# Entry of the output stage: who makes the low parts of the output weights, and when

## The chip, the cores and the metric

The kernel runs on one core of a Trainium2 chip. The metric is the time of one execution on the device in microseconds. Five engines work side by side, each through its own list of instructions: TensorE (PE in the profile), VectorE (DVE), ScalarE (ACT), GpSimd (POOL) and SyncE (SP), which here only issues transfers. They meet by semaphores: an instruction waits until a counter has reached a value, and adds to a counter when it is done.

## The reference

One layer of a diffusion backbone, for 256 prompt tokens and 2048 sample tokens, width 1024, float32:

```
h = RMSNorm(x) * (1 + scale1) + shift1
q, k, v, r, decays, conv inputs = split(h @ w_in)
A = per-head RMSNorm(gated linear attention, both directions) * norm_g * silu(r)   # 512 wide, 4 heads
B = silu(LayerNorm(depthwise conv, width 31, of ga * sigmoid(gg)))                  # 512 wide
x = x + gate1 * (concat(A, B) @ w_out)                                              # w_out: 1024 x 1024
h = RMSNorm(x) * (1 + scale2) + shift2
x = x + gate2 * ExpertChoiceMoE(h)                                                  # 16 experts
y = RMSNorm(x)
```

Outputs are y of both token sets and the final states of the two attention scans of the prompt.

## The kernel before

**Products in two parts.** Each float32 operand of a large product is split into a high part (a rounded copy, `ACT.Copy` by ScalarE into a tile of type fp32r) and a low part (the operand less its high part, a `tensor_tensor` subtraction by VectorE or GpSimd). `three` (lines 1649 to 1652) then runs three matmuls: high by high, high by low, low by high.

**Stages.** Stage 2 projects the tokens and runs attention and convolution, first for the prompt and then for four blocks of 512 sample tokens. It parks its results in HBM (`park_q`, `park_s` for states, `park_o`, `park_r`, `park_c` for the convolution). Stage 3 takes them back in five groups m = 0 to 4: group 0 is the prompt (256 tokens, two tiles of 128), groups 1 to 4 are the blocks, last block first (512 tokens, four tiles each). It finishes the norms, multiplies by the output weights, adds the residual and computes the router's logits. Stage 4 runs the experts. The change is at the entry of stage 3, in the `prologue` of each engine, which prepares group 0 and the output weights; `stage3(m)` then computes group m while it prepares group m + 1.

**Order.** Nothing is scheduled by a planner: each engine's instructions run in the order in which the code writes them. What stands behind a waiting instruction on its engine waits too.

**The output weights.** `wo_hl[:, 0, k, :]` and `wo_hl[:, 1, k, :]` are the high and low part of k-slice k (k = 0 to 7, each 128x1024). SyncE loads w_out in four transfers of two slices (1 MB each) into the three buffers `wstage` (which later hold x rows, scaled rows and h2 of stage 3); the fourth goes into buffer 0 once slices 0 and 1 are split. `wo_hi(k)` (line 1139, ScalarE) makes a high part and raises `r_wh`. `wo_lo(k)` (line 2711, VectorE) waits for it, makes the low part and raises `r_wl`.

**VectorE's prologue** (lines 2716 to 2730): `centre(0)` (2627), `taps` 108 to 117 of the last block's convolution (2560), `add_inter(0)` (2635), `taps` 118 to 123, `wo_lo` 0 to 3, `gate_heads(0)` (2642, four multiplications of 128x256), `wo_lo` 4 and 5, `stat_recips(0)` (2647 a reciprocal, 2649 its low part), `wo_lo` 6 and 7, `scale_all(0)` (2657 the four heads, 2663 the convolution's four quarters), a copy (2730).

**ScalarE's prologue**: squares of the convolution (1067), `wo_hi` 0 and 1, the gate rows (1149), `wo_hi` 2 and 3, squares of the heads (1074), `wo_hi` 4 and 5, `stat_roots(0)` (1079, a square root of sums that TensorE made), `stat_hi(0)` (1087, waits for the reciprocal), `wo_hi` 6 and 7, `cat_his(0)` (1100 high parts of attention, 1093 the convolution's silu, 1100 high parts of the convolution).

**GpSimd** makes the low parts of attention and convolution, `cat_lo` (1454). Before its first one in stage 3 it has only four memsets (1469 to 1473).

**TensorE's prologue**: sums of squares (1922, 1926), `spread(0)` (1939, spreads the reciprocals over the partitions into PSUM). Then `out_half(g, q)` multiplies tile g by half q of the weights, 24 matmuls of 128x512; the first one waits for `r_wl` slice by slice. Behind the 48 matmuls of tile 0 come `conv_mean(1)` (1914, waits for `park_c` of group 1) and `inter(1)` (1904, the product of queries and states, waits for `back_states(1)`, line 2611, on VectorE, which waits for the parked states).

**SyncE** at this place, in its order: three loads of w_out, `load_r(0)`, the store of the prompt's state, `store_c(final)` (622, the last block's convolution, waits for all its taps), a wait for two low parts, the fourth load of w_out (718), `load_qS(1)` (633 queries, 637 and 638 states), `load_r(1)`, a wait for all eight low parts, the x rows of tiles 0 and 1 (673), then `load_c(1)` and `load_o(1)` (645, 651), which wait for the low parts of group 0.

Of the kernel before, what the change touches and what calls it, by code (L numbers as in the profile page):

```python
# [41 lines left out]
TAPS = 4 * CW  # L42
# [56 lines left out]
def hybrid_layer(nc, x_prompt, x_sample, state_gla_fwd, state_gla_bwd, c, c_ctx, norm_mix_g, norm_ffn_g,  # L99
# [3 lines left out]
    f32, f32r, bf16, u32 = mybir.dt.float32, mybir.dt.float32r, mybir.dt.bfloat16, mybir.dt.uint32  # L103
    f16 = mybir.dt.float16
    ALU = mybir.AluOpType
# [3 lines left out]
    with ctx:  # L109
# [66 lines left out]
        with ExitStack() as st:  # L176
            wo_hl = group(st, "wo_hl", [128, 2, KC, D], f32r)
# [213 lines left out]
        r_x2st, r_h2st = [sem("r_x2st0"), sem("r_x2st1")], [sem("r_h2st0"), sem("r_h2st1")]  # L391

        P_AFF, P_COPY = 5, 7

        def upto(eng, sig_, n):

            eng.wait_ge(sig_.sem, sig_.base + n)
# [127 lines left out]
        def _(sp):  # L525
# [192 lines left out]
            sp.dma_start(wstage[0], wo_v[3]).then_inc(r_wo[0].sem, 16)  # L718
            load_qS(1)
            load_r(1)  # L720
            sp.wait_ge(r_wl, 8)
            load_x3(0)
            load_x3(1)
            for m in range(NBLK + 1):
# [106 lines left out]
        def _(act):  # L831
# [244 lines left out]
            def stat_roots(m):  # L1076
                act.wait_ge(r_st, 2 * m + 2)
                wait_pos(act, r_bc, 5 * m)
                act.activation(W3["rs"][0:64, 0:T3[m]], psum[7][0:64, 0:T3[m]], ACT.Sqrt, bias=eps[0:64, :],
                               scale=1.0 / DV).then_inc(r_sr, 1)  # L1080

            def stat_hi(m):
                act.wait_ge(r_rc, m + 1)
                wait_pos(act, r_bc, 5 * m)
                if m == 0:
                    act.wait_ge(r_sel, 4)
                act.activation(spread_rs[0:64, 0:T3[m]], W3["rs"][0:64, 0:T3[m]], ACT.Copy).then_inc(r_sh.sem, 1)
# [48 lines left out]
            def prologue():  # L1136
                def wo_hi(k):
                    upto(act, r_wo[k // 2 % 3], 32 if k >= 6 else 16)
                    act.activation(wo_hl[:, 0, k, :], wstage[k // 2 % 3][:, k % 2, :], ACT.Copy).then_inc(r_wh, 1)

                for j in range(16):
                    act.activation(diag[:, j, :], ident[:, :], ACT.Copy, scale=mod[:, 16 + j % 8, j // 8:j // 8 + 1])\
                       .then_inc(r_dg, 1)
                conv_squares(0)
                wo_hi(0)
                wo_hi(1)
                for j in range(4):
                    act.wait_ge(r_gt, j + 1)
                    act.activation(gt1[:, j // 2, 512 * (j % 2):512 * (j % 2) + 512], psum[j][:, :], ACT.Copy)\
                       .then_inc(r_gr, 1)  # L1150
                wo_hi(2)
                wo_hi(3)
                head_squares(0)
                upto(act, r_mt, 1)
                act.activation(mod2_rows, psum[4][0:2 * KC, 0:256], ACT.Copy).then_inc(r_mt.sem, 1)
                wo_hi(4)
                wo_hi(5)
                stat_roots(0)
                stat_hi(0)
                wo_hi(6)  # L1160
                wo_hi(7)
                cat_his(0)
# [205 lines left out]
        def _(pool):  # L1368
# [105 lines left out]
            def routing_constants():  # L1474
# [27 lines left out]
                for out, pattern, cm in ((iota_a[:, :], [[16, 16]], 0), (iota_b[:, :], [[1, 16]], 0),  # L1502
                                         (iota_p[:, :], [[1, CAPP]], 0), (lat_id[:, :], [[128, NL]], 1),
                                         (pr_id[:, :, :], [[128, 2], [0, 2]], 1)):
                    chain(pool.iota(out, pattern, base=0, channel_multiplier=cm, allow_small_or_imprecise_dtypes=True))

            for m in range(NBLK + 1):
                for half in range(2):
                    if m == 0:
                        final.wait(pool, s_conv if half == 0 else s_cstr, TAPS if half == 0 else s_cstr.l)  # L1510
                    for t in range(min(NT3[m], 3)):
                        cat_lo(m, t, half)
                if NT3[m] == 4:
                    cat_lo(m, 3, 0)
                    cat_lo(m, 3, 1)
                if m == 1:
                    routing_constants()
# [120 lines left out]
        def _(pe):  # L1638
# [305 lines left out]
            def out_half(g, q, k0=0, k1=KC):  # L1944
                m = M_OF[g]
                t = g - G3[m]
                if g >= 2 and k0 == 0:
                    pe.wait_ge(r_y, 2 * (g - 2) + q + 1)
                elif q == 0 and k0 == 0:
                    pe.wait_ge(r_gr, 4)  # L1950
                for k in range(k0, k1):
                    if g == 0 and q == 0:
                        pe.wait_ge(r_wl, k + 1)
                    if q == 0 and k % 4 == 0:
                        upto(pe, r_lo, piece(m, t, k // 4))
                    a = cat_hl[:, :, k, 128 * t:128 * t + 128]
                    last = three(psum[2 * (g % 2) + q][:, :], a[:, 0], a[:, 1], wo_hl[:, 0, k, 512 * q:512 * q + 512],
                                 wo_hl[:, 1, k, 512 * q:512 * q + 512], k == 0, k == KC - 1)
                if k1 == KC:
                    last.then_inc(r_T.sem, 1)  # L1960
# [369 lines left out]
        def _(dve):  # L2330
# [368 lines left out]
            def prologue():  # L2699
# [14 lines left out]
                centre(0)  # L2714
                taps(final, LATE, 118)
                add_inter(0)
                taps(final, 118, TAPS)
                wo_lo(0)
                wo_lo(1)
                wo_lo(2)  # L2720
                wo_lo(3)
                gate_heads(0)
                wo_lo(4)
                wo_lo(5)
                stat_recips(0)
                wo_lo(6)
                wo_lo(7)
                scale_all(0)
                dve.wait_ge(r_br, 1)
                dve.tensor_copy(brow_w, psum[5][:, 0:2 * NE]).then_inc(r_wr, 1)  # L2730

# [538 lines left out]
```

## Time and profile before

| | us |
|---|---|
| median of 3 runs | 2403.95 (2400.47 to 2404.53) |
| the profiled execution | 2401.75, of which the profiled span is 2400.0 |
| TensorE busy in the span | 2240.2 (93%) |
| VectorE, ScalarE, GpSimd busy | 1667.6, 1193.9, 721.8 |

Times in the rows are microseconds from the start of the span. Engines wait for each other, so an engine's busy time says little by itself; the timelines show an instruction's start and length and, in brackets, the idle time ahead of it and what ended it. Tiles of the three stages bear the names of their regions: work_proj (stage 2), work_out (stage 3), work_exp (stage 4); bank is a PSUM bank. PEclk is the clock granted to TensorE, 1.00 for 2.4 GHz and 0.50 for 1.2 GHz. The DMA share is the mean busy share of the 16 DMA engines.

### The profile page before, as it was taken

To read this page: it belongs to the slowest core of one execution; us is meant where nothing else is said; L and a number is where in the kernel's file an instruction comes from. 1 tells how busy PE (TensorE), PEld (TensorE's weight loads), DVE (VectorE), ACT (ScalarE), POOL (GpSimd) and SP (SyncE) were. 2 spreads that over 40 slices of the span, in tenths; PEclk is the share of its full clock that TensorE was granted. 3 is DMA by queue.
4 is the path that set the end of the run, shared out by engine and by line. 5 is a ranking of instruction groups with operands and counts; after the bars stand their busy time and mean duration, and the time that the engine had idled before them with its cause. 6 is when DMAs were issued, how large, how long until landed. Compare 5 with 4: busy or idle time off the path is not lost.

```text
span 2400.0 us, 43832 instructions
## 1 busy us (share of the span) xinstructions
PE 2240.2 (93%) x16687; PEld 2053.6 (86%) x16687; DVE 1667.6 (69%) x2936; ACT 1193.9 (50%) x1935; POOL 721.8 (30%) x663
## 2 busy tenths in 40 slices
PE   4889999999996899975999999999999999999995
PEld 4778878788885677753999999999999999999995
DVE  2879979799788766767666655665656656666585
ACT  3765363553524454432545554555445554555574
POOL 2000000000001311101254455544554455544551
PEclk8999999999997999987999999999999999999998
DMA  8986677657747566355476677667776677666986
GB/s 297 347 292 217 219 245 248 238 184 273 221 131 265 166 203 198 102 178 139 151 206 193 184 199 214 188 183 200 198 214 183 176 213 198 207 184 185 299 253 241
DMA packets 289654, 505.79 MB, mean 211 GB/s; under 512 B 26178, under 2 KB 232895, under 8 KB 273921
## 3 DMA queue, kind: packets, MB, share of 16 engines
q1 hardware_dynamic: 249622, 376.39, 47.9%
q0 software_dynamic: 39424, 126.64, 19.5%
q8 instruction: 78, 1.28, 0.2%
q10 hardware_dynamic: 490, 1.16, 0.1%
q14 instruction: 40, 0.32, 0.0%
HBM read 405.61 MB, written 98.53 MB: 210 GB/s over the span
## 4 chain that ended last, share of the span: by engine, by line
PE 61%; DVE 5%; ACT 2%; issue 1%; DMA 1%; POOL 0%; SPq 0%; DVEq 0%; POOLq 0%; ACTq 0%
PE bank L1650 19%; PE bank L1652 19%; PE bank L1651 19%; PE bank L1904 1%; DVE work_exp L2921 1%; DVE work_proj L2560 1%; PE bank L1970 1%; PE bank L1914 1%; PE bank L1922 1%; DMA work_exp<-x_rows 0%; POOL cat_hl L1454 0%; PE bank L1979 0%; PE bank L2213 0%; DVE wo_hl L2711 0%; ACT hl_exp L1231 0%
## 5 line engine op out<-in xcount | busy, mean ns | idle before, releaser
L1650 PE MATMUL bank<-act_hl_exp,hl_exp 128*128 128x288 f32 x3072 | 909.2, 296 | 12.2 <-DVE hl_exp L3100 7.3
L1651 PE MATMUL bank<-act_hl_exp,hl_exp 128*128 128x288 f32 x3072 | 906.5, 295 | 0.0
L1652 PE MATMUL bank<-act_hl_exp,hl_exp 128*128 128x288 f32 x3072 | 905.0, 295 | 0.0
L1650 PEld LDWEIGHTS bank<-act_hl_exp,hl_exp 128*128 128x128 f32 x3072 | 576.7, 188 | 13.7 <-DVE hl_exp L3100 9.8
L1652 PEld LDWEIGHTS bank<-act_hl_exp,hl_exp 128*128 128x128 f32 x3072 | 578.6, 188 | 0.0
L1651 PEld LDWEIGHTS bank<-act_hl_exp,hl_exp 128*128 128x128 f32 x3072 | 577.3, 188 | 0.0
L3100 DVE TENSOR_TENSOR hl_exp<-work_exp,hl_exp 128x1024 fp32r<-128x1024 f32 x192 | 231.3, 1226 | 206.1 <-ACT hl_exp L1231 206.1
L3100 DVE TENSOR_TENSOR hl_exp<-raw_exp,hl_exp 128x1024 fp32r<-128x1024 f32 x192 | 232.0, 1225 | 193.3 <-ACT hl_exp L1231 193.3
L2560 DVE SCALAR_TENSOR_TENSOR work_proj<-work_proj,wcv 128x392 f32<-128x392 f32 (+12 forms) x600 | 338.8, 635 | 1.2
L1231 ACT ACTIVATE hl_exp<-work_exp 128x1024 fp32r<-128x1024 f32 x192 | 199.2, 1054 | 201.3 <-PE bank L1652 201.3
L1231 ACT ACTIVATE hl_exp<-raw_exp 128x1024 fp32r<-128x1024 f32 x192 | 198.5, 1052 | 161.5 <-PE bank L1652 161.5
L1565 POOL TENSOR_TENSOR act_hl_exp<-work_exp,act_hl_exp 128x288 fp32r<-128x288 f32 x128 | 155.5, 1234 | 360.0 <-ACT act_hl_exp L1257 360.0
L1588 POOL DMA_INDIRECT x_rows<-work_exp x135 | 241.6, 1790 | 60.3 <-issue 36.0
L1650 PE MATMUL bank<-act_hl_proj,hl_proj 128*128 128x512 f32 (+1 forms) x640 | 239.4, 374 | 6.0 <-DVE hl_proj L2387 6.0
L1651 PE MATMUL bank<-act_hl_proj,hl_proj 128*128 128x512 f32 (+1 forms) x640 | 234.9, 367 | 0.0
L1652 PE MATMUL bank<-act_hl_proj,hl_proj 128*128 128x512 f32 (+1 forms) x640 | 234.7, 367 | 0.0
L1427 POOL DMA_DIRECT2D hl_proj<-park_w x80 | 43.3, 542 | 602.0 <-PE bank L1652 511.2
L1553 POOL DMA_INDIRECT work_exp<-h_rows,work_exp x135 | 162.0, 1200 | 50.0 <-issue 38.3
L1242 ACT ACTIVATE work_exp<-work_exp 128x256 f32<-128x256 f32 x240 | 102.3, 497 | 90.3 <-DVE work_exp L3111 64.0
L1650 PEld LDWEIGHTS bank<-act_hl_proj,hl_proj 128*128 128x128 f32 x640 | 123.3, 193 | 27.2 <-issue 8.7
L1652 PEld LDWEIGHTS bank<-act_hl_proj,hl_proj 128*128 128x128 f32 x640 | 123.0, 192 | 19.6
L1651 PEld LDWEIGHTS bank<-act_hl_proj,hl_proj 128*128 128x128 f32 x640 | 123.3, 193 | 17.8
(411 smaller groups left out, 3317.4 us busy)
## 6 DMA issues: line engine op xcount, KB each, us to landing
hl_proj<-park_w POOLq DMA_DIRECT2D x80, 1024.0 KB, 6.1
raw_exp<-in_w_e_gate_dram SPq DMA_DIRECT2D x32, 1024.0 KB, 5.9
raw_exp<-in_w_e_up_dram SPq DMA_DIRECT2D x32, 1024.0 KB, 5.8
work_exp<-in_w_e_gate_dram SPq DMA_DIRECT2D x32, 1024.0 KB
work_exp<-in_w_e_up_dram SPq DMA_DIRECT2D x32, 1024.0 KB, 6.5
raw_exp<-in_w_e_down_dram SPq DMA_DIRECT2D x32, 1024.0 KB, 6.2
work_exp<-in_w_e_down_dram SPq DMA_DIRECT2D x32, 1024.0 KB, 5.8
park_w<-hl_proj SPq DMA_DIRECT2D x8, 2048.0 KB, 12.0
```

What stands on the lines that cost most here:

```text
L1231: act.activation(half_out(j, q, 0, is_last(e)), half_in(src, j, q, is_last(e)), ACT.Copy).then_inc(s_hi, 1)
L1242: last = act.activation(h32e[:, k % 2, a:z], xT[:, k % 2, a:z], ACT.Identity, scale=A2q[:, cnd, k:k + 1], bias=sh2q[:, cnd, k:k + 1])
L1427: pool.dma_start(hl[:, j % 2, q], park_w[j, :, q]).then_inc(s_w[j % 2][q].sem, 16)
L1553: pool.indirect_dma_start(xg[:, b, :], None, h2_rows[:, :], bass.IndirectOffsetOnAxis(ap=ids_g[:, b:b + 1], axis=0)).then_inc(e_gat, 16)
L1565: pool.tensor_tensor(xe_hl[:, 1, k, :], h32e[:, k % 2, :], xe_hl[:, 0, k, :].bitcast(f32), ALU.subtract)\
L1588: pool.indirect_dma_start(x2_quarters[:, :], bass.IndirectOffsetOnAxis(ap=ids_s[:, b:b + 1], axis=0), y_t[:, b, :], None, compute_op=ALU.a ...
L1650: pe.matmul(out, lh, rh, start=first, stop=False)
L1651: pe.matmul(out, lh, rl, start=False, stop=False)
L1652: return pe.matmul(out, ll, rh, start=False, stop=last_)
L1904: ins = pe.matmul(psum[7 - h % 2][v:v + 64, 64 * cc:64 * cc + 64], S3[:, cc + 1, 128 * h + v:128 * h + v + 64], part("q", m, h)[:, 64 * cc ...
L2560: dve.scalar_tensor_tensor(out=ac[:, :, a0:a1], in0=uu[:, :, a0 + off:a1 + off], scalar=wcv[:, ct, w:w + 1], in1=ac[:, :, a0:a1], op0=ALU. ...
L3100: dve.tensor_tensor(half_out(j, q, 1, is_last(e)), half_in(src, j, q, is_last(e)), half_out(j, q, 0, is_last(e)).bitcast(f32), ALU.subtrac ...
```

## The change

GpSimd makes the low parts of slices 2 to 5, with a counter of its own (`r_wlp`, on a semaphore that has reached 20 by then), in order and ahead of its first `cat_lo`; each waits for its high part. VectorE makes the low parts of slices 0 and 1 ahead of its last six taps, and those of 6 and 7 behind `scale_all(0)`. ScalarE makes high part 4 between `stat_roots(0)` and `stat_hi(0)`, and high part 5 behind it. TensorE and SyncE wait for both counters.

```diff
--- before.py
+++ after.py
@@ -391,6 +391,7 @@
         r_x2st, r_h2st = [sem("r_x2st0"), sem("r_x2st1")], [sem("r_h2st0"), sem("r_h2st1")]
 
         P_AFF, P_COPY = 5, 7
+        r_wlp = Sig(s_cst, 0, 0, 20)
 
         def upto(eng, sig_, n):
 
@@ -718,7 +719,8 @@
             sp.dma_start(wstage[0], wo_v[3]).then_inc(r_wo[0].sem, 16)
             load_qS(1)
             load_r(1)
-            sp.wait_ge(r_wl, 8)
+            sp.wait_ge(r_wl, 4)
+            upto(sp, r_wlp, 4)
             load_x3(0)
             load_x3(1)
             for m in range(NBLK + 1):
@@ -1153,10 +1155,10 @@
                 head_squares(0)
                 upto(act, r_mt, 1)
                 act.activation(mod2_rows, psum[4][0:2 * KC, 0:256], ACT.Copy).then_inc(r_mt.sem, 1)
+                stat_roots(0)
                 wo_hi(4)
+                stat_hi(0)
                 wo_hi(5)
-                stat_roots(0)
-                stat_hi(0)
                 wo_hi(6)
                 wo_hi(7)
                 cat_his(0)
@@ -1504,6 +1506,10 @@
                                          (pr_id[:, :, :], [[128, 2], [0, 2]], 1)):
                     chain(pool.iota(out, pattern, base=0, channel_multiplier=cm, allow_small_or_imprecise_dtypes=True))
 
+            for k in range(2, 6):
+                pool.wait_ge(r_wh, k + 1)
+                pool.tensor_tensor(wo_hl[:, 1, k, :], wstage[k // 2 % 3][:, k % 2, :], wo_hl[:, 0, k, :].bitcast(f32),
+                                   ALU.subtract).then_inc(r_wlp.sem, 1)
             for m in range(NBLK + 1):
                 for half in range(2):
                     if m == 0:
@@ -1949,8 +1955,10 @@
                 elif q == 0 and k0 == 0:
                     pe.wait_ge(r_gr, 4)
                 for k in range(k0, k1):
-                    if g == 0 and q == 0:
-                        pe.wait_ge(r_wl, k + 1)
+                    if g == 0 and q == 0 and 2 <= k < 6:
+                        upto(pe, r_wlp, k - 1)
+                    elif g == 0 and q == 0:
+                        pe.wait_ge(r_wl, k + 1 if k < 2 else k - 3)
                     if q == 0 and k % 4 == 0:
                         upto(pe, r_lo, piece(m, t, k // 4))
                     a = cat_hl[:, :, k, 128 * t:128 * t + 128]
@@ -2714,18 +2722,14 @@
                 centre(0)
                 taps(final, LATE, 118)
                 add_inter(0)
-                taps(final, 118, TAPS)
                 wo_lo(0)
                 wo_lo(1)
-                wo_lo(2)
-                wo_lo(3)
+                taps(final, 118, TAPS)
                 gate_heads(0)
-                wo_lo(4)
-                wo_lo(5)
                 stat_recips(0)
+                scale_all(0)
                 wo_lo(6)
                 wo_lo(7)
-                scale_all(0)
                 dve.wait_ge(r_br, 1)
                 dve.tensor_copy(brow_w, psum[5][:, 0:2 * NE]).then_inc(r_wr, 1)
```

## Rows read from the trace of the kernel before

**Rows 1.** The page: chain that ended last, share of the span by engine.
```profile
PE 61%; DVE 5%; ACT 2%; issue 1%; DMA 1%; POOL 0%; SPq 0%; DVEq 0%; POOLq 0%; ACTq 0%
```

**Rows 2.** Timeline, VectorE: start us, length us, engine, line, op, output<-inputs, count [idle before<-releaser].
```profile
741.72 3.36 DVE L2560 SCALAR_TENSOR_TENSOR work_proj<-work_proj,wcv 128x408 f32<-128x408 f32 x6
...
744.99 4.62 DVE L2711 TENSOR_TENSOR wo_hl<-work_out,wo_hl 128x1024 fp32r<-128x1024 f32 x4
...
749.53 1.43 DVE L2642 TENSOR_TENSOR work_out<-work_out 128x256 f32<-128x256 f32 x4
...
753.15 1.73 DVE L2647 RECIPROCAL work_out<-work_out 64x256 f32<-64x256 f32 x1
...
758.59 0.87 DVE L2657 SCALAR_TENSOR_TENSOR work_out<-work_out,col,bank 128x256 f32<-128x256 f32 x2
...
760.89 1.42 DVE L2663 TENSOR_TENSOR work_out<-work_out,bank 128x256 f32<-128x256 f32 x4 [0.28 <-PE bank L1939]
...
766.96 0.60 DVE L2605 COPY work_out<-carry 64x512 f32<-64x512 f32 x1 [4.55 <-DMA work_out<-park_s]
...
767.59 10.42 DVE L2611 SCALAR_TENSOR_TENSOR work_out<-work_out,dec 64x128 f32<-64x128 f32 x32
```

**Rows 3.** Timeline of ScalarE, from 744 to 762 us.
```profile
744.06 2.01 ACT L1139 ACTIVATE wo_hl<-work_out 128x1024 fp32r<-128x1024 f32 x2
...
751.03 0.47 ACT L1079 ACTIVATE work_out<-bank,eps 64x256 f32<-64x256 f32 x1
...
760.65 1.15 ACT L1100 ACTIVATE cat_hl<-work_out 128x512 fp32r<-128x512 f32 x2 [3.42 <-DVE work_out L2657]
```

**Rows 4.** Timeline of GpSimd, from 728 to 764 us.
```profile
761.43 2.50 POOL L1454 TENSOR_TENSOR cat_hl<-work_out,cat_hl 128x512 fp32r<-128x512 f32 x2 [33.89 <-ACT cat_hl L1100]
```

**Rows 5.** Timeline of TensorE's matmuls, from 746 to 780 us.
```profile
746.43 0.40 PE L1926 MATMUL bank<-work_out 128*32 128x256 f32 x1 [2.56 <-ACT work_out L1074]
...
748.09 1.06 PE L1926 MATMUL bank<-work_out 128*32 128x256 f32 x2
...
762.84 0.77 PE L1650 MATMUL bank<-wo_hl,cat_hl 128*128 128x512 f32 x1 [1.99 <-POOL cat_hl L1454]
...
776.41 3.59 PE L1914 MATMUL bank<-work_out,ones 128*128 128x512 f32 x8
```

**Rows 6.** Timeline of SyncE's queue: the issues of transfers, 745 to 769 us.
```profile
745.11 0.34 SPq L622 DMA_DIRECT2D park_c<-work_proj  x1
...
747.37 0.37 SPq L718 DMA_DIRECT2D work_out<-in_w_out_dram  x1
...
768.73 0.33 SPq L645 DMA_DIRECT2D work_out<-park_c  x1
```

**Rows 7.** Stretches: length, busy us of each engine (instructions), PEclk, DMA share, GB/s.
```profile
745.50:775.00 29.50, 20.76 (x77) 15.54 (x78) 23.17 (x47) 13.89 (x22) 5.21 (x4) 0.65 0.99 315
...
747.60:768.00 20.40, 12.59 (x39) 9.30 (x36) 14.24 (x23) 11.81 (x17) 4.52 (x4) 0.50 1.00 282
```

**Rows 8.** Transfers issued at 745.11, 747.37, 768.73: KB, us from issue to landing.
```profile
park_c<-work_proj SPq DMA_DIRECT2D x1, 1024.0 KB, 4.1
...
work_out<-in_w_out_dram SPq DMA_DIRECT2D x1, 1024.0 KB, 5.7
...
work_out<-park_c SPq DMA_DIRECT2D x1, 1024.0 KB, 6.2
```

**Rows 9.** Timelines of GpSimd and VectorE, at 43 us and from 813 us.
```profile
43.27 2.49 POOL L1422 TENSOR_TENSOR act_hl_proj<-work_proj,act_hl_proj 128x1024 fp32r<-128x1024 f32 x1 [1.94 <-ACT act_hl_proj L898]
...
44.18 2.67 DVE L2378 TENSOR_TENSOR act_hl_proj<-work_proj,act_hl_proj 128x1024 fp32r<-128x1024 f32 x1 [0.62 <-ACT act_hl_proj L898]
...
813.91 6.55 POOL L1454 TENSOR_TENSOR cat_hl<-work_out,cat_hl 128x512 fp32r<-128x512 f32 x5 [2.20 <-ACT cat_hl L1100]
...
815.31 1.38 DVE L2611 SCALAR_TENSOR_TENSOR work_out<-work_out,dec 64x128 f32<-64x128 f32 x1
```

**Rows 10.** Groups of ScalarE by line: table load, mean ns, idle before, releaser.
```profile
L855 ACT ACT_TABLE_LOAD x1 | 1.3, 1283 | 15.8 <-DVE col L2333 15.8
```

## Prediction

> **What bounds the kernel now.** I began with the chain of work that ended last. TensorE has 61% of it [rows 1], so the entry of stage 3 matters only as far as it holds TensorE up. Then I read the timelines of this entry, engine by engine, to see what releases TensorE.
>
> VectorE runs without a break: the six last convolution taps from 741.72 to 745.0, low parts 0 to 3 from 744.99 (4.62 us), the head gating, then low parts 4 and 5, the reciprocal, low parts 6 and 7, and the head scaling from 758.59 [rows 2]. ScalarE makes the first high part of attention at 760.65 [rows 3], GpSimd its low part from 761.43 [rows 4], and TensorE starts on the output matmuls at 762.84, having idled 1.99 us for GpSimd [rows 5]. The 48 matmuls of tile 0 and what follows run without a gap until conv_mean(1), 776.41 to 780.0 [rows 5]. This is the chain that the change wants shorter.
>
> A second chain runs beside it. SyncE waits for the last tap before it stores the convolution (issue 745.11), and behind that store stand, in its queue, the fourth part of the output weights (747.37) and all the loads of group 1 [rows 6]. From 745.5 to 775 the DMA engines are busy 0.99 of the time [rows 7]. They serve SyncE's transfers in the order of issue: the store lands after 4.1 us, at 749.2, the fourth part at 753.1, the convolution of group 1 at 774.9 [rows 6, 8]. The parked states of group 1 stand two transfers ahead of the x rows in the same queue: VectorE idles 4.55 us for it until 766.96 and needs 0.60 and 10.42 us for the backward states [rows 2], to 778.04. TensorE reaches conv_mean(1) only 1.5 us after its data landed (776.41 less 774.9), and the head product behind it at 780.0, 1.9 us after the states. So whatever the first chain gains, this second one takes over within 1.5 us; and whatever delays the store beyond that delays TensorE.
>
> **The change part by part.**
>
> *VectorE.* Low parts 0 and 1 move ahead of the taps: 2 x 1.155 = 2.31 us (4.62 / 4) [rows 2]. The first begins at 741.72, as its high part was ready. The taps then begin at 744.03 and end at 747.35 if nothing disturbs them (6 in 3.3 us). That alone moves the store by 2.35 us.
>
> *GpSimd.* It gets four differences of 128x1024. The trace has one such: 2.49 us [rows 9]. The first may start when ScalarE has made high part 2, 1.0 us after 744.06, at 745.1 [rows 3]. That is among the taps. What this does to VectorE is seen twice. While the 128x1024 difference ran from 43.27 to 45.76, a VectorE difference of the same size, started at 44.18, took 2.67 us instead of 1.16 (it ended 1.1 us behind GpSimd's). And among the five differences that GpSimd makes from 813.91, VectorE's 64x128 state step took 1.38 us (815.31), against 10.42 / 32 = 0.33 us in rows 2, so one VectorE step passed for each of GpSimd's (6.55 / 5 = 1.31 us) [rows 2, 9]. VectorE's work whose second input is a PSUM bank did not suffer: four at 760.89 in 1.42 us while GpSimd worked from 761.43 [rows 2, 4]. The taps and the gating have both inputs in SBUF, so I take them as blocked.
>
> The Trainium skill (SBUF — State Buffer, section Who interferes with whom) says the same as a rule: VectorE with two SBUF inputs and a GpSimd instruction that reads SBUF contend, and the second fully blocks until the first is done. The trace agrees (2.67 us at 44.18). If the two ran freely side by side, the taps would cost nothing more; that is rival A.
>
> Played through: GpSimd begins at 745.15, after tap 2. Tap 3 waits until 747.65 and runs 0.55; GpSimd's second runs 748.2 to 750.7; taps 4, 5, 6 run from 750.7 to 752.35. If tap 3 wins the first race, the sum is the same: two blocks of 2.5 us inside the taps. So the taps end at 744.03 + 3.3 + 5.0 = 752.35. GpSimd's third difference needs high part 4. ScalarE now makes it after the roots, which need TensorE's sums at 749.2 and a table load of 1.28 us [rows 10]. The load stands behind its wait where that can be seen (15.8 us of idle ahead of one) [rows 10]. The sums are two matmuls of 0.5 us at 748.1 [rows 5]; the root takes 0.5 us and the high part 1.0 [rows 3]. That gives 749.2 + 1.28 + 0.5 + 1.0 = 752.0: just too late for the taps, but it blocks the gating by another 2.5 us. Gating ends at 754.85 + 1.43 = 756.3, the reciprocal (1.73) at 758.0, the head scaling starts at about 759.6, 1.0 us later than now. The low parts taken out of this chain (4 x 1.16 us) are so given back by 3 blocks of 2.5 us.
>
> *SyncE.* The store is issued at 752.45, 7.3 us later than 745.11. The engines lie idle meanwhile. Everything behind moves by 7.3 us, less up to 0.6 us of thin traffic between the issues before: 6.7 to 7.3. The fourth part lands at 760.5 (752.45 + 4.1 + 3.9). ScalarE needs 2 x 1.0 us for high parts 6 and 7 ahead of the attention's, which so comes at 762.5 instead of 760.65 [rows 3]: TensorE starts 1.8 us later than 762.84 and comes free for conv_mean(1) at 778.2. VectorE's low parts 6 and 7, now behind the scaling, are ready by 768.3; TensorE wants them 18 matmuls after its start, about 772. No cost. GpSimd's fourth difference (759.5 to 762.0) is done before the attention's high part. No cost. The new waits of SyncE (x rows of group 0) fall under transfers that queue until 776; no cost.
>
> *Where it decides.* The convolution of group 1 lands at 774.9 + 6.7 to 7.3 = 781.6 to 782.2, so conv_mean(1) starts 5.2 to 5.8 us later than 776.41. The other input agrees: the state lands at 773.7 to 774.3, the backward states end 11.1 us later, 784.8 to 785.4, against a head product at 780.0 before: 4.8 to 5.4 later. I take 5.5. Nothing behind it is tied to an earlier time: all loads and steps of the later groups are released by steps of this one, so the delay stays to the end.
>
> *The clock.* TensorE will idle about 4 us ahead of conv_mean(1). Its granted clock was 0.50 (1.2 GHz) from 747.6 to 768 [rows 7], after 2.56 us of idle ahead of 746.43 [rows 5]. conv_mean's eight matmuls take 3.59 us at 2.4 GHz; at half of it they cost up to 3.5 us more, at best nothing. I take the middle, 1.6.
>
> **Sum:** 5.5 + 1.6 = +7.1 us. The profiled execution took 2401.75 us (span 2400.0 and 1.75 around it), which becomes 2408.9. The median of the runs is 2403.95, 2.2 above it, so I forecast 2411.0. Its own range: 4.8 + 0 to 5.8 + 3.5, so 2408.8 to 2413.3.
>
> **The rivals.**
>
> A. *No block.* GpSimd and VectorE run side by side on the taps. For it: TensorE's and PSUM-fed work is undisturbed; against it rows 9. Then the taps end at 747.35, the store goes 2.35 us later, the convolution lands at 777.3, 0.9 us later than 776.41; the states end at 780.4, 0.4 later than 780.0. TensorE waits from 773.3 on (as in C), so the clock may cost 0 to 3.5 as well. Time 2404.9, up to 2408.
>
> B. *A third block inside the taps.* If high part 4 is ready before 751.8 (the table loaded ahead of the wait), GpSimd's third difference gets in before taps 5 and 6. One more 2.5 us: +9.6, 2413.6. Rows 10 speak against it.
>
> C. *The change does what it says* and the second chain does not bind. High parts 6 and 7 wait for the fourth part (753.1 + 2.4 = 755.5), the attention's high part comes at 757.5 instead of 760.65: 3.1 us gained, 2400.8; TensorE starts at 759.7 and is through with tile 0 at 773.3 (776.41 less 3.1). It decides this way only if conv_mean's data land before 773.3, though the store goes later and the DMA engines are full [rows 7]. I see nothing for that.
>
> **How the numbers follow.** Forecast 0.62, A 0.22, B 0.12, C 0.04. The predicted time is the forecast's, 2411.0. The range goes from A to just above B, 2404.9 to 2414.0: outside lie C, the lowest times of A and the upper half of B, below 2 in 10. About 0.2% (4.8 us) is what a measurement of this kernel can tell from no change, so the border is at 2408.8. Slower: the forecast less its low end (0.57), B (0.12) and a little of A (0.02), 0.71. Within: A (0.20), C (0.03), the forecast's low end (0.04), 0.27. Faster 0.02.
>
> **What would show it.** In the profile of the changed kernel: two of the last six taps last some 3 us each, a gating step some 2.5; the convolution's store is issued near 752.4; conv_mean(1) starts near 782 behind a wait for the DMA of the convolution, with a granted clock of 0.50 for some us. It is wrong if the taps keep 0.55 us each, if the store is issued by 748, or if the transfers behind it land no later than before.

## The result

| | before | after |
|---|---|---|
| median of 6 runs, us | 2399.93 (2397.47 to 2404.53) | 2410.42 (2406.9 to 2413.86) |
| profiled execution, us | 2401.75 (span 2400.0) | 2412.79 (span 2411.1) |

The ratio is 1.0042 (95% interval 1.0027 to 1.0057), so the change costs 10.1 us (6.5 to 13.7). The time forecast, 2411.0, is near the measured one; the change forecast, 7.1 us, is too small by 3.0. The two don't say the same because the kernel before came out 4.0 us lower in six runs than in the three that the forecast stood on. The change in us is what the reasons have to answer for, and there a rival that I had given 0.12 is what happened. The kernel before was timed again beside the experiments: its medians there are 2401.86, 2400.24 and 2401.82, and 2410.42 is 8.6 to 10.2 us above these; the traces below give 9.6.

**The chain that ended last, in the changed kernel** (start us, length us, what), at the entry of stage 3:

```profile
741.96 2.27 DVE wo_hl L2719 x2
744.22 4.37 DVE work_proj L2568 x5
...
751.08 2.71 DVE work_proj L2568
...
753.80 0.34 SPq L623
...
754.19 7.20 DMA work_out<-in_w_out_dram
...
761.41 2.00 ACT wo_hl L1141 x2
...
771.19 13.12 DMA work_out<-park_c
...
784.35 5.40 PE bank L1920 x8
```

Read it from below. TensorE's conv_mean(1) waits for the convolution of group 1 (13.12 us from issue to landing); its issue waits for GpSimd's low parts of the prompt, these for ScalarE, which makes high parts 6 and 7 first and waits for the fourth weights (7.20 us), and these stand in SyncE's queue behind the store at 753.80, which waits for the last tap. In the kernel before, the chain went through the norms to TensorE's first output matmul. It now goes through the store and two transfers. The 13.12 us are mostly queueing: from the store's issue to the landing of the convolution the DMA engines are busy 0.99 of the time, and this takes 30.5 us, against 29.8 in the kernel before (745.11 to 774.9).

The three taps that lost time, in VectorE's timeline, and what GpSimd did then:

```profile
745.79 2.73 DVE L2568 SCALAR_TENSOR_TENSOR work_proj<-work_proj,wcv 128x400 f32<-128x400 f32 x1
...
748.45 2.71 DVE L2568 SCALAR_TENSOR_TENSOR work_proj<-work_proj,wcv 128x392 f32<-128x392 f32 x1
...
751.08 2.70 DVE L2568 SCALAR_TENSOR_TENSOR work_proj<-work_proj,wcv 128x392 f32<-128x392 f32 x1
```

```profile
745.36 2.73 POOL L1511 TENSOR_TENSOR wo_hl<-work_out,wo_hl 128x1024 fp32r<-128x1024 f32 x1 [17.68 <-ACT wo_hl L1141]
...
748.06 2.67 POOL L1511 TENSOR_TENSOR wo_hl<-work_out,wo_hl 128x1024 fp32r<-128x1024 f32 x1
...
751.01 2.35 POOL L1511 TENSOR_TENSOR wo_hl<-work_out,wo_hl 128x1024 fp32r<-128x1024 f32 x1 [0.28 <-ACT wo_hl L1141]
```

Each tap ends 0.4 us behind the end of a difference of GpSimd's: 748.52 behind 748.09, 751.16 behind 750.73, 753.78 behind 753.36. In these rows it gets its turn only when that difference is through, and the next difference then takes the turn ahead of the next tap. The six taps take 9.64 us, against 3.36 in [rows 2]. The other lines of TensorE and VectorE that answer to [rows 5] and [rows 2] (SyncE's, for [rows 6], stand in the chain above: 753.80, 754.19 and 771.19):

```profile
766.13 0.76 PE L1656 MATMUL bank<-wo_hl,cat_hl 128*128 128x512 f32 x1 [5.51 <-POOL cat_hl L1456]
...
784.35 5.40 PE L1920 MATMUL bank<-work_out,ones 128*128 128x512 f32 x8 [4.50 <-DMA work_out<-park_c]
789.68 1.15 PE L1910 MATMUL bank<-work_out 128*64 128x64 f32 x32
```

```profile
776.43 0.42 DVE L2613 COPY work_out<-carry 64x512 f32<-64x512 f32 x1 [11.46 <-DMA work_out<-park_s]
```

TensorE's late start (766.13 against 762.84) is the store's doing too. VectorE's head scaling is not late: it begins 17.3 us behind the second pair of head additions (line 2643, at 741.06), against 17.7 before. ScalarE waits for the fourth weights:

```profile
761.41 2.00 ACT L1141 ACTIVATE wo_hl<-work_out 128x1024 fp32r<-128x1024 f32 x2 [3.24 <-DMA work_out<-in_w_out_dram]
```

The landings behind 753.80 and 771.19, and four stretches (the columns of [rows 7]):

```profile
park_c<-work_proj SPq DMA_DIRECT2D x1, 1024.0 KB, 5.0
...
work_out<-park_c SPq DMA_DIRECT2D x1, 1024.0 KB, 13.1
```

```profile
745.50:775.00 29.50, 17.64 (x63) 13.00 (x64) 17.32 (x21) 13.92 (x22) 15.59 (x8) 0.60 0.70 190
...
753.80:784.00 30.20, 16.07 (x53) 12.08 (x53) 16.38 (x42) 8.91 (x13) 8.02 (x5) 0.71 0.99 307
...
780.00:784.30 4.30, 0.00 (x0) 0.00 (x0) 4.16 (x15) 0.00 (x0) 0.00 (x0) 1.00 1.01 417
...
785.00:788.00 3.00, 3.00 (x5) 1.20 (x4) 1.80 (x6) 0.00 (x0) 0.00 (x0) 0.50 0.04 16
```

The DMA share from 745.5 to 775 fell from 0.99 to 0.70: the engines had nothing to do until the store came. TensorE idles 4.50 us. Its granted clock still stands at 1.00 from 780 to 784.3, without a matmul, and is 0.50 (1.2 GHz) from 785 to 788, when the matmuls run again: conv_mean(1) takes 5.40 us instead of 3.59.

What is lost there stays lost. The head product is 9.75 us later (789.68 against 779.93), and the first matmul of the experts 9.8 us later: 1134.4 to 1144.2, in the group of these matmuls of before and of after (nanoseconds least/median/most, first and last start in us):

```profile
L1650 PE MATMUL bank<-act_hl_exp,hl_exp x3072: 288/295/607, 1134.4 to 2378.2; 128*128 128x288 f32 x192
```

```profile
L1656 PE MATMUL bank<-act_hl_exp,hl_exp x3072: 288/295/609, 1144.2 to 2388.8; 128*128 128x288 f32 x192
```

### The profile page after: what moved, and what is told of

The parts are those of the page before. It is cut to its first block, busy times and chain, and to the rows that moved or that the text cites. A ratio compares the mean times of both kernels' runs of the same rounds, so it can differ in the third digit from the quotient of the medians.

```text
span 2411.1 us, 43833 instructions
## 1 busy us (share of the span) xinstructions
PE 2243.5 (93%) x16687; PEld 2056.0 (85%) x16687; DVE 1669.3 (69%) x2932; ACT 1193.9 (50%) x1935; POOL 732.9 (30%) x667
## 3 DMA queue, kind: packets, MB, share of 16 engines
q0 software_dynamic: 39424, 126.64, 19.5%
## 4 chain that ended last, share of the span: by engine, by line
PE 60%; DVE 4%; DMA 3%; ACT 1%; issue 1%; POOL 1%; SPq 0%; DVEq 0%; ACTq 0%; POOLq 0%
PE bank L1656 19%; PE bank L1658 18%; PE bank L1657 18%; DMA out_dram<-work_exp 1%; PE bank L1910 1%; DMA work_out<-park_c 1%; PE bank L1920 1%; PE bank L1978 1%; DVE work_exp L2925 1%; DVE work_proj L2568 1%; PE bank L1928 1%; DVE work_exp L3188 0%; POOL cat_hl L1456 0%; DMA work_exp<-x_rows 0%; PE bank L2149 0%
## 5 line engine op out<-in xcount | busy, mean ns | idle before, releaser
L2568 DVE SCALAR_TENSOR_TENSOR work_proj<-work_proj,wcv 128x392 f32<-128x392 f32 (+12 forms) x600 | 345.2, 647 | 1.2
L1658 PEld LDWEIGHTS bank<-act_hl_proj,hl_proj 128*128 128x128 f32 x640 | 122.9, 192 | 19.5
```

Source lines behind the costliest of these rows:

```text
L1658: return pe.matmul(out, ll, rh, start=False, stop=last_)
L2568: dve.scalar_tensor_tensor(out=ac[:, :, a0:a1], in0=uu[:, :, a0 + off:a1 + off], scalar=wcv[:, ct, w:w + 1], in1=ac[:, :, a0:a1], op0=ALU. ...
```

## The experiments

Theory: GpSimd's differences block VectorE's taps whole instructions at a time, so the store at the head of all transfers of group 1 goes out late, and TensorE waits for the last of them and then runs for a while at half its clock. Main rival: the norms' chain, or rather TensorE's late start on the output matmuls (766.13, 3.3 us later), is what costs. The trace of the changed kernel speaks against it already: TensorE waits 4.50 us for the data after the late start.

Executions enter the stage up to 1.2 us earlier or later, so I measure each trace from the start of VectorE's second pair of head additions (line 2635; 740.91 in the kernel before) to the start of the head product, the matmul behind conv_mean(1). This is 39.0 us before. "First matmul" is TensorE's first output matmul, counted from the pair as well. Each trace is one execution, and executions of one kernel differ by some 10 us over the whole (kernel before, 2395.85 to 2407.08), so the traces say where time is lost and the timed column says how surely. e2 and e5 ran once each, for their traces: 2402.4 and 2411.21 us, beside medians of 2401.86 and 2400.24 for the kernel before.

| kernel | pair, us | first matmul, after the pair | head product, us | between | against before | timed against before, us (interval) |
|---|---|---|---|---|---|---|
| before | 740.91 | 21.9 | 779.93 | 39.0 | | |
| changed | 741.06 | 25.1 | 789.68 | 48.6 | +9.6 | +10.1 (6.5 to 13.7) |
| e1, GpSimd after the taps | 741.06 | 19.5 | 782.89 | 41.8 | +2.8 | +2.2 (-0.5 to 5.0) |
| e2, GpSimd only writes | 740.46 | 18.1 | 782.58 | 42.1 | +3.1 | |
| e3, store behind all loads | 739.72 | 21.6 | 785.86 | 46.1 | +7.1 | +4.8 (2.4 to 7.2) |
| e4, lows first, no GpSimd | 741.51 | 25.2 | 784.79 | 43.3 | +4.3 | +2.6 (0 to 5.5) |
| e5, high part 4 later | 742.14 | 23.2 | 789.97 | 47.8 | +8.8 | |
| e6, TensorE kept busy | 741.19 | 22.4 | 787.84 | 46.7 | +7.6 | +9.1 (5.5 to 12.5) |
| e7, store behind the queries | 739.98 | 21.5 | 780.35 | 40.4 | +1.4 | +1.2 (-1.2 to 3.6) |
| e8, first chain alone | 739.94 | 17.4 | 777.08 | 37.1 | -1.9 | -0.2 (-2.9 to 2.4) |
| c2, both chains | 740.60 | 16.3 | 775.02 | 34.4 | -4.6 | -1.0 (-3.6 to 1.4) |
| c2 again | 740.94 | 16.7 | 775.79 | 34.9 | -4.2 | -3.8 (-7.0 to -1.0) |

(Times in us are the ratio less one, by 2400.) The loss doesn't follow TensorE's start: in e1 and e2 it starts 2.5 and 3.8 us sooner than before and 2.8 and 3.1 us are still lost. In both, conv_mean(1) starts 1.0 and 0.6 us later than before, behind a wait for its data.

**Does the block make the loss?** GpSimd's work unchanged, only begun behind the last tap (on the changed kernel):

```diff
+            final.wait(pool, s_conv, TAPS)
             for k in range(2, 6):
```

> The changed kernel, but GpSimd begins its four low parts only when the last tap of the convolution is done. Theory (GpSimd blocks VectorE's taps, and the store behind the taps is the head of all transfers of group 1): the six taps take 3.3 us again, the store is issued at 747.5 instead of 753.8, conv_mean(1) starts at 777.3 and the head product behind it at about 781; time 1 us above the kernel before (about 2401), at most 4 if the clock falls. The gating and the head scaling stay late (scaling at 758 to 759), TensorE's first output matmul at about 763. Rival (the late start of TensorE's output matmuls, 766.1 instead of 762.8, makes the loss, the store does not matter): the time follows that start, so 0 to 1 us above before as well; the two part in the run with the store moved.

```profile
744.14 3.36 DVE L2569 SCALAR_TENSOR_TENSOR work_proj<-work_proj,wcv 128x408 f32<-128x408 f32 x6
747.41 1.43 DVE L2651 TENSOR_TENSOR work_out<-work_out 128x256 f32<-128x256 f32 x4
...
752.21 1.42 DVE L2658 TENSOR_TENSOR reset<-work_out,reset 64x256 fp32r<-64x256 f32 x1 [0.48 <-ACT reset L1089]
```

```profile
747.58 3.46 POOL L1512 TENSOR_TENSOR wo_hl<-work_out,wo_hl 128x1024 fp32r<-128x1024 f32 x1 [19.90 <-DVE work_proj L2569]
```

```profile
777.57 5.40 PE L1921 MATMUL bank<-work_out,ones 128*128 128x512 f32 x8 [3.85 <-DMA work_out<-park_c]
782.89 1.15 PE L1911 MATMUL bank<-work_out 128*64 128x64 f32 x32
```

The taps are at 3.36 us again and 6.8 of the 9.6 us are gone. Start of conv_mean(1) and size are as expected, the clock's share with it (5.40 us after 3.85 of idle). The norms' chain I had wrong: head scaling at 754.31 and TensorE's first output matmul at 760.52, where I had said 758 to 759 and 763. It was not late at all. GpSimd's first difference came up at 747.58, with the gating begun at 747.41, and this time GpSimd waited: its difference took 3.46 us and the four gating steps kept their 1.43. So which engine goes first, and after how many instructions of the other, is not the same everywhere; among the taps it was one for one. The chain was blocked elsewhere: the difference of 64x256 at 752.21 took 1.42 us instead of 0.42, beside GpSimd.

**Is it what GpSimd reads?** The same four tiles, filled with zeros:

```diff
-                pool.tensor_tensor(wo_hl[:, 1, k, :], wstage[...], wo_hl[:, 0, k, :]..., ALU.subtract)
+                pool.memset(wo_hl[:, 1, k, :].bitcast(f32), 0.0)
```

> The changed kernel, but GpSimd fills its four low parts with zeros instead of subtracting (the low parts of slices 2 to 5 are left out of the result): it writes the same tiles at the same places and reads nothing. Theory (VectorE's second input and GpSimd's reads share one way): the taps take 3.3 to 3.6 us, store issued at 747.5 to 748, no tap longer than 0.7 us. Rival (any GpSimd work beside the taps slows them, by writes or by its mere presence): taps of over 1 us remain.

```profile
743.53 3.36 DVE L2567 SCALAR_TENSOR_TENSOR work_proj<-work_proj,wcv 128x408 f32<-128x408 f32 x6
```

```profile
744.73 1.90 POOL L1511 MEMSET wo_hl<- 128x1024 f32 x2 [17.74 <-ACT wo_hl L1141]
```

Two fills of GpSimd lie wholly among the taps, and the taps take 3.36 us. Writing the same tiles beside VectorE costs it nothing; the differences, which read as well, do. The Trainium skill (SBUF — State Buffer, Who interferes with whom) says that a VectorE instruction with two SBUF inputs contends with a GpSimd instruction that reads SBUF, and not with one that only writes it. The trace agrees (3.36 us). The fills are shorter (0.95 us each) than the differences and are another instruction, but a block of even 0.95 would show. That 3.1 us remain here too is 0.6 us of later data and the clock: conv_mean(1) took 6.06 us, after 3.96 us of idle time.

**Does the store's place decide?** First the store behind all loads of group 1:

```diff
-            store_c(final, NBLK)
             sp.wait_ge(r_wl, 2)
...
             load_r(1)
+            store_c(final, NBLK)
```

> The changed kernel, but in SyncE's queue the store of the last convolution stands behind the fourth weights and all loads of states, queries and gates of group 1 (still ahead of the load that reads it). The taps stay blocked and end at about 753.8. Theory (what costs is the place of the store at the head of the transfers): the parked states land near 764, VectorE's backward states are done by 776, conv_mean(1) starts within 1 us of 776.4; time within 2 us of the kernel before, some 9 us below the changed one. Rival (the late norms' chain and TensorE's late start cost): TensorE starts no earlier than 763 to 766 and 3 to 10 us of loss remain.

```profile
769.75 2.55 POOL L1456 TENSOR_TENSOR cat_hl<-work_out,cat_hl 128x512 fp32r<-128x512 f32 x2 [6.37 <-DMA park_c<-work_proj]
```

```profile
771.16 0.77 PE L1656 MATMUL bank<-wo_hl,cat_hl 128*128 128x512 f32 x1 [4.39 <-POOL cat_hl L1456]
...
782.33 3.60 PE L1920 MATMUL bank<-work_out,ones 128*128 128x512 f32 x8
```

A miss: 7.1 us remain, and neither theory had the reason. The states did come early (backward states done at 776.6), but GpSimd waits for this store before its low parts of the convolution, which the code says and I had overlooked: 6.37 us for the DMA of park_c, and TensorE 4.39 us for GpSimd in the middle of the first tile. TensorE's start was as early as before (21.6 us after the pair), so that the rival has no part in these 7.1 us. The store has two customers. So it was put where both can live, behind the fourth weights and the queries and ahead of the states (the edit on SyncE; `load_qS` is split in two for it):

```diff
-            store_c(final, NBLK)
             sp.wait_ge(r_wl, 2)
             sp.dma_start(wstage[0], wo_v[3]).then_inc(r_wo[0].sem, 16)
-            load_qS(1)
+            load_q(1)
+            store_c(final, NBLK)
+            load_S(1)
```

> The changed kernel, with the store of the last convolution behind the fourth weights and the queries of group 1 but ahead of the states, so that GpSimd, which waits for this store before its low parts of the convolution (the cause of 4.4 us of TensorE's idle time in the run with the store further back), has it by 762. The taps stay blocked (done at 751 to 754). Theory (the order of the transfers decides): the DMA engines work again from 744, the states land at 767 to 768, the convolution of group 1 at 775 to 776, TensorE waits for neither, conv_mean(1) starts at 776 to 777.5 without a fall of the clock, the head product at 780 to 781; time 0 to 2 us above the kernel before. Rival (the blocked norms' chain itself costs): conv_mean(1) not before 780 and 4 us or more above before.

```profile
743.05 9.64 DVE L2576 SCALAR_TENSOR_TENSOR work_proj<-work_proj,wcv 128x408 f32<-128x408 f32 x6
```

```profile
776.72 3.70 PE L1928 MATMUL bank<-work_out,ones 128*128 128x512 f32 x8 [1.29 <-DMA work_out<-park_c]
```

The taps are blocked as fully as in the changed kernel (9.64 us), yet the loss is 1.4 us instead of 9.6. The DMA engines work while the taps are held up (share 0.61 from 743.2 to 752.7, against 0.00 from 745.5 to 753.8 in the changed kernel), and only the order of SyncE's queue was changed. This shows that the block costs through the store's place. It doesn't part the store from TensorE's late start, for the fourth weights came early too and TensorE started 21.5 us after the pair; that is settled by the 4.50 us of waiting in the changed kernel and by e1, where TensorE starts sooner than before and time is lost all the same.

**Does a late store cost without GpSimd?** On the kernel before, VectorE's low parts 0 to 3 ahead of the taps:

```diff
+                wo_lo(0) ... wo_lo(3)
                 taps(final, 118, TAPS)
-                wo_lo(0) ... wo_lo(3)
```

> The kernel before, with the low parts 0 to 3 ahead of the last six taps on VectorE and nothing else changed; GpSimd has no part in it. Theory (a late store costs whatever makes it late): taps end at 750.7, the store is issued 5.6 us later than before, conv_mean(1) starts 4.1 us later, at 780.5, and the clock may add up to 3.5: 4 to 7.5 us above before. Rival (only GpSimd's work costs, or only the norms' chain, which is unchanged in length here): within 1 us of before.

```profile
751.42 0.34 SPq L622 DMA_DIRECT2D park_c<-work_proj  x1
```

```profile
781.16 3.70 PE L1914 MATMUL bank<-work_out,ones 128*128 128x512 f32 x8 [0.80 <-DMA work_out<-park_c]
```

Store 5.7 us later (6.3 less the 0.6 by which this execution ran late), loss 4.3 us, at the low end of what was expected, because TensorE waited only 0.80 us and the clock held (3.70). I had called the norms' chain unchanged here, and it is not: the fourth weights stand behind the store, high parts 6 and 7 wait for them (1.95 us), and TensorE starts 3.2 us later (25.2 us after the pair). So most of the 4.2 us by which conv_mean(1) is late would have been lost by this start alone. A late store costs without GpSimd, by two ways that end within 0.8 us of each other. The timed difference, 2.6 us, agrees within its interval but is too wide to add anything.

**How large is one block?** On the changed kernel, high part 4 behind the reciprocal's high part, so that GpSimd's third difference comes too late for taps and gating:

```diff
                 stat_roots(0)
-                wo_hi(4)
                 stat_hi(0)
+                wo_hi(4)
                 wo_hi(5)
```

> The changed kernel, but high part 4 is made after the reciprocal's high part and not between the roots and it, so GpSimd's third difference cannot begin among the taps or the gating. Theory (each GpSimd difference holds up the VectorE step behind it for its whole length): the six taps take 8.2 us (two blocks) instead of 9.64, the store is issued at about 752.4, 1.4 us earlier than in the changed kernel, and the head product behind conv_mean(1) at about 788.3 instead of 789.7; the gating takes 1.43 us. Rival (taps are slowed by a rate, not by whole instructions): the taps keep about 9.6 us.

```profile
745.21 7.54 DVE L2568 SCALAR_TENSOR_TENSOR work_proj<-work_proj,wcv 128x408 f32<-128x408 f32 x6
752.68 1.42 DVE L2650 TENSOR_TENSOR work_out<-work_out 128x256 f32<-128x256 f32 x4
```

```profile
783.33 6.71 PE L1920 MATMUL bank<-work_out,ones 128*128 128x512 f32 x8 [4.94 <-DMA work_out<-park_c]
```

Two blocks make the taps 4.2 us longer (7.54 less 3.36), three 6.3 (9.64). So one costs 2.1 us, not 2.5: a caught tap takes 2.7 us, as long as the differences are apart, and a free one 0.55. The store goes out 2.1 us sooner than in the changed kernel (10.6 against 12.7 after the pair), the head product only 0.8: here conv_mean took 6.71 us, after 4.94 us of idle time.

**Is the rest the clock?** On the changed kernel, nine matmuls without use ahead of conv_mean(1):

```diff
+                if m == 0:
+                    pe.wait_ge(r_cn, 4)
+                    for _ in range(9):
+                        pe.matmul(psum[6][:, :], ones[:, :], wo_hl[:, 0, 0, 0:512].bitcast(f32), start=True, stop=True)
                 conv_mean(prep)
```

> The changed kernel, with nine matmuls of 128x512 without use (into the bank that conv_mean(1) clears) put ahead of conv_mean(1), about 4 us of work where TensorE idles 4.5 us. Theory (1.8 us of the loss is the clock that falls in this idle time): conv_mean(1) still starts at 784.4 but takes 3.6 us instead of 5.4, the head product comes 1.8 us earlier, time some 2 us below the changed kernel. Rival (the clock falls for another reason, or conv_mean is slow by contention): conv_mean(1) keeps 5.4 us.

```profile
744.26 7.55 DVE L2572 SCALAR_TENSOR_TENSOR work_proj<-work_proj,wcv 128x408 f32<-128x408 f32 x6
751.73 3.56 DVE L2654 TENSOR_TENSOR work_out<-work_out 128x256 f32<-128x256 f32 x4
```

```profile
784.32 3.60 PE L1920 MATMUL bank<-work_out,ones 128*128 128x512 f32 x8
```

```profile
776.60:787.90 11.30, 11.30 (x29) 4.81 (x28) 7.09 (x25) 0.00 (x0) 0.00 (x0) 1.00 0.51 210
```

With TensorE busy, the granted clock stays at 1.00 and conv_mean takes 3.60 us instead of 5.40. But the nine took 7.9 us, twice what I had planned, and now stood in the way themselves, while in this execution GpSimd's third difference fell on the gating (taps 7.55, gating 3.56), so the data came sooner than in the changed kernel. The size of the clock's part is shown by the length of conv_mean; the total of this run is not clean, and its timed difference to the changed kernel (9.1 against 10.1) is within the noise. Over all traces: idle of 0.80 to 1.63 us ahead of conv_mean leaves it at 3.70, idle of 3.85 to 4.94 makes it 5.40 to 6.71.

**What was the aim worth?** A version with the norms' chain truly shortened: taps first; GpSimd makes low part 2 behind the gating and 3 behind the reciprocal's low part; VectorE makes 4 to 7 behind the scaling; ScalarE makes high parts 6 and 7 behind the convolution's. SyncE's queue stays as before. Of the edit, GpSimd's part:

```diff
-            for k in range(2, 6):
+            for k in (2, 3):
+                if k == 2:
+                    pool.wait_ge(r_or, 4)
+                else:
+                    upto(pool, r_sl, 1)
                 pool.wait_ge(r_wh, k + 1)
```

> The faster version's order of work on VectorE, ScalarE and GpSimd (no GpSimd difference among the taps, TensorE's first output matmul at 757 instead of 762.8), with SyncE's queue as in the kernel before: store at 745, fourth weights, queries, states, gates, x rows, and only then the convolution of group 1. Theory (the second chain caps the gain and its wait lets the clock fall): TensorE is through with tile 0 at 770.6 to 771, waits 4 us for the convolution of group 1, which lands at 775, conv_mean takes 5.4 to 6.7 us, the head product comes at 780 to 782 against 779.9 before: nothing gained, 0 to 2 us lost, though TensorE starts 6 us earlier. Rival (the first chain is what bounds): the head product at 774 to 775, 4 to 5 us below before.

```profile
757.29 0.77 PE L1668 MATMUL bank<-wo_hl,cat_hl 128*128 128x512 f32 x1 [1.98 <-POOL cat_hl L1464]
...
773.45 3.70 PE L1932 MATMUL bank<-work_out,ones 128*128 128x512 f32 x8 [1.63 <-DMA work_out<-park_c]
```

TensorE starts 4.6 us sooner (17.4 us after the pair against 21.9) and the head product comes 1.9 us sooner. Neither 0 to 2 lost nor 4 to 5 gained: the cap is where the slack of the second chain puts it (the forecast had read 1.5 and 1.9 us), but the wait was 1.63 us and not 4, so the clock held. I had left out that VectorE's last low parts hold TensorE up a little, and that TensorE starts at half clock all the same. Timed, the version can't be told from before.

Then the same with SyncE's queue changed too: states of group 1 ahead of the store (the DMA engines have nothing to do from 742.5 to 745.5 in the kernel before), convolution and attention of group 1 ahead of gates and x rows. Of the edit, SyncE's queue:

```diff
+            sp.wait_ge(r_in, 8)
+            load_S(1)
             store_c(final, NBLK)
             sp.wait_ge(r_wl, 2)
             sp.dma_start(wstage[0], wo_v[3]).then_inc(r_wo[0].sem, 16)
-            load_qS(1)
+            load_q(1)
+            load_oc(1)
             load_r(1)
```

> A version that follows from the theory. VectorE: taps first, then low parts 0 and 1, gating, reciprocal, scaling, low parts 4 to 7. GpSimd: low part 2 only after the gating, 3 only after the reciprocal's low part, so it meets no tap. ScalarE: high part 4 ahead of the reciprocal's, 5 behind, 6 and 7 behind the high parts of the convolution. SyncE: states of group 1 ahead of the store (the DMA engines idle there from 742 to 745), then store, fourth weights, queries, then convolution and attention of group 1 ahead of gates and x rows. Theory: store issued at 745, TensorE's first output matmul at 757 to 759 instead of 762.8, states and queries landed by 765, conv_mean(1) at 771 to 773, the head product at 776 instead of 780: 3 to 4 us below before. Rival (another wait takes over, or the clock falls in the gap): within 1.5 us of before.

The profile gave all that was expected, the timed runs (1.0 us) did not settle it. So once more:

> The same kernel as c2_both_chains, for a narrower interval: its profile has the head product 4.9 us and the span 5.4 us below before, its timed runs only 1.0 (interval 3.6 below to 1.4 above). If the profile is typical: 4 to 5 us below before. If not: 0 to 2 us below, and the profiled execution was a fast one of a wide spread.

```profile
757.65 0.76 PE L1670 MATMUL bank<-wo_hl,cat_hl 128*128 128x512 f32 x1 [1.98 <-POOL cat_hl L1466]
...
772.01 3.60 PE L1934 MATMUL bank<-work_out,ones 128*128 128x512 f32 x8
775.79 1.15 PE L1924 MATMUL bank<-work_out 128*64 128x64 f32 x32 [0.18 <-issue]
```

TensorE waits for nothing at conv_mean(1), and 4.2 to 4.6 us are gone from the trace in both executions. Timed, the second series has it 3.8 us below before (1.0 to 7.0), the first 1.0 (3.6 below to 1.4 above). The first interval takes in no change, and doesn't reach the 4.6 of its own trace; only the second is clear of no change. That it beats the changed kernel is shown; that it beats the kernel before is likely, by an amount that stays open, between 1 and 4 us.

## Where the prediction was right and where not, point by point

*What bounds.* Right. Two chains with 1.5 and 1.9 us of slack between them: e8 gained 1.9 where the first alone was shortened by 4.6, and c2 gained 4.2 to 4.6 where both were.

*GpSimd blocks the taps.* Right in kind (e1, e2), wrong in number and size. The gating, on which I had put the third difference, kept its 1.42 us, and the head scaling began at 758.35, not 759.6. I had two blocks of 2.5 us among the taps and a third on the gating; the changed kernel's trace has three of 2.1 among the taps. The step that failed, for the number of blocks, is ScalarE's: I let the table load wait for TensorE's sums, from the one row where that could be seen [rows 10]. It does not have to:

```profile
747.85 1.28 ACT L1081 ACT_TABLE_LOAD   x1
749.51 0.47 ACT L1081 ACTIVATE work_out<-bank,eps 64x256 f32<-64x256 f32 x1 [0.38 <-PE bank L1932]
749.88 1.04 ACT L1141 ACTIVATE wo_hl<-work_out 128x1024 fp32r<-128x1024 f32 x1
```

The load runs at 747.85, the root starts right behind the sums at 749.51, after 0.38 us of waiting for TensorE, and high part 4 is there at 750.9 instead of 752.0. That was rival B's condition, to which I gave 0.12. The race is close: in the traces of e3 and e6 the third difference fell on the gating as forecast, in those of the changed kernel and e7 on a tap. So what happened is rival B and not the forecast. Its price, +9.6 us, is also nearer to the change measured (10.1) than mine (7.1); that 2411.0 is nearer to 2410.42 than B's 2413.6 is due to the lower time of the kernel before, which is luck. B in its turn had a block too large (2.5 against 2.1) and nothing for what the transfers added.

*The store.* Forecast 7.3 us later, measured 8.5 (12.7 against 4.2 us after the pair). All from the third block: 3 x 2.1 + 2.3 = 8.6.

*The transfers behind.* I subtracted up to 0.6 us for thin traffic; in fact 0.8 were added. The states came 9.3 us later and the convolution as well. The store itself took 5.0 us, not 4.1, with the weights right behind it. So conv_mean(1) started 7.9 us later, not 5.5: this term was mis-sized, by 1.2 for the store and 1.2 for the transfers.

*The clock.* Forecast 1.6, measured 1.8 (5.40 less 3.59). That is luck in part: 1.6 was put near the middle of 0 and 3.5 (which is 1.75) without a reason for the middle, and after similar waits the other traces show 1.8 (e1), 2.5 (e2) and 3.1 us (e5).

*What I costed at nothing.* TensorE's start at 766.13 (forecast 764.6) cost nothing, since it waited 4.50 us afterwards. Its path was the one forecast: the fourth weights, ScalarE's high parts 6 and 7, the attention's high part. Low parts 6 and 7, the x rows and GpSimd's fourth difference held up nobody. That the delay stays to the end was right: +9.75 at the head product, +9.8 at the experts' first matmul.

*The sum.* 7.9 + 1.8 = 9.7 us against the 7.1 forecast, and 10.1 timed. The place where it is decided, the wait and the clock were the forecast's, with one term 2.4 us too small: half of that is rival B's third block, half is what the transfers added.

*Rivals.* A is what e1 shows: its price was 0.9 and up to 3.5 for the clock, measured 2.8. C fails by the second chain; e8 shows where it stops.

## What to carry to other kernels

Before work is moved to an idle engine, look at what the others do in that stretch and where their operands lie: here GpSimd's reads and VectorE's instructions with two SBUF inputs held each other up by whole instructions, so a 2.4 us instruction placed beside short ones made each tap that it caught a long one (2.7 us for 0.55). Then look at who waits for those short ones. Here it was a store that a whole queue of transfers stood behind, and moving that store behind two of these transfers (e7) gave back 8.2 of the 9.6 us in the traces, more than the 4.6 us of work that the change had moved.

## What was not expected of the hardware

- ScalarE's table load ran ahead of the wait of the instruction that needs it (747.85, root at 749.51), though another load had stood behind its wait [rows 10]. Which of the two happens is not explained by these runs.
- GpSimd's fills of 128x1024 (0.95 us each) beside VectorE's taps cost these nothing, its differences of the same tiles 2.1 us each.
- Either side can pay: in e1 GpSimd's difference took 3.46 us beside the gating and the gating nothing more. In e6 both paid: GpSimd's two differences of 128x512 took 3.49 us instead of 2.50 [rows 4], and VectorE's two low parts beside them 4.55 instead of 2.36:

```profile
762.14 3.49 POOL L1456 TENSOR_TENSOR cat_hl<-work_out,cat_hl 128x512 fp32r<-128x512 f32 x2 [1.36 <-ACT cat_hl L1102]
```

```profile
762.16 4.55 DVE L2723 TENSOR_TENSOR wo_hl<-work_out,wo_hl 128x1024 fp32r<-128x1024 f32 x2
```
